# Differential attention in a two-block kernel: the first map left unscaled, the heads held with tokens on partitions, one root and one reciprocal for all heads

## The chip, the cores and the metric

The kernel runs on one core of a Trainium2 chip. The metric is the device time of one execution in microseconds (us). All arithmetic is float32; a large matmul is made of three float32r matmuls on high and low halves of its operands.

## The reference, cut to what matters

The program computes two transformer blocks for 256 latent tokens with 256 context tokens. The change concerns one layer of the first block, differential attention with 8 heads. A head has two score maps (m = 0, 1) of 64 dimensions each and 128 value dimensions. In the reference:

```python
def diff_attend(q, k, v, lam, scale):
    s = jnp.einsum('bqhmd,bkhmd->bhmqk', q, k).astype(jnp.float32) * scale
    p = jax.nn.softmax(s, axis=-1)
    p = p[:, :, 0] - lam * p[:, :, 1]
    return jnp.einsum('bhqk,bkhv->bqhv', p.astype(v.dtype), v)

def out(o):
    o = rms_norm_gain(o, subln_g) * (1.0 - lambda_init)      # over the 128 values of one head, eps 1e-6
    return o.reshape(b, n, DIFF_HEADS * DIFF_DV) @ w_out
```

With e0 and e1 the exponentials of the two maps and s0 and s1 their row sums, the weights of a token are e0/s0 - lam * e1/s1. The norm that follows divides each head's output by its own root mean square, so a factor common to the whole row of a head (such as 1/s0) drops out of it, up to the eps.

## The kernel before, in words

**Program.** The five engines run hand-written streams side by side and meet at semaphores (`S("name")`; `own(...)` issues an instruction and then waits for it on the same engine). Weights come in tiles of 128x1024, one DMA each, through four slots. For every tile ScalarE writes the high half (`hi`, L1159 to L1165), VectorE the low half (`lo`, L1536 to L1540), and then the matmuls may use it. ScalarE reuses a slot of high halves once the matmuls of the tile three before it are done (`tile_done`); the reload of a raw slot waits for the low half (SyncE, L406). `gemm_cols` (L629 to L646) is the output projection: for each of 8 weight tiles k, 8 banks of PSUM get 3 matmuls of 256 columns each. At the end of the last tile each bank is released (`bank_done`), and VectorE adds it to the residual (`residual`, L1611).

**Attention stage.** There are 16 tiles u: 8 heads times 2 blocks of 128 queries. All engines run one software pipeline over u:

- TensorE (L814 to L841): the two score matmuls of tile u (keys 0 to 511 in the free dimension), the four transposes of the mixed map of tile u-2, and the four matmuls with the values of tile u-3. The values are the stationary operand here, so a head's output stands with its 128 value dimensions on partitions and 256 tokens in the free dimension, in bank 6 or 7.
- VectorE (L1844 to L1871): the row maxima of both maps of tile u out of PSUM (L1852), each followed by a small multiply (L1853); then for tile u-1 the reciprocal of both row sums (L1859), the product with -lambda (L1860), the first map scaled by its reciprocal (L1863), and the second map scaled and added (L1864), after which VectorE waits for its own result (L1866). Every second u it also copies a finished head out of PSUM (L1871).
- ScalarE (L1322 to L1336): two exponentials with row sums of tile u, and the copy of the transposed map of tile u-2 from PSUM.

**Norm of the heads.** After the loop, per head: ScalarE squares the head (L1342), TensorE sums over the partitions with a matrix of ones (L846), VectorE scales the 128x256 sums and adds eps (L1877), ScalarE takes the root of 128x256 (L1346), VectorE takes the reciprocal of 128x256 (L1882) and multiplies head, gain and reciprocal (L1883). Then ScalarE rounds the head to the high half (L1349) and GpSimd takes the low half (L500 to L503). The output projection (L849) needs each head only when it comes to its k. `do_var` at 8 (L848) comes before its first matmul.

What follows is the residual, the squares of the next norm, and the second feed-forward layer, whose first weight tiles are converted during the projection.

## Time and profile before

| | |
|---|---|
| device time, median of 3 runs | 3301.37 us (3298.73 to 3304.07) |
| the profiled execution: its own time | 3304.16 us |
| the profiled execution: span | 3302.4 us |
| mean granted clock of TensorE | 0.962 |
| busy share of the span | TensorE 93%, weight load 76%, VectorE 64%, ScalarE 36%, GpSimd 6% |
| attention stage, from the end of the value projection to the first matmul of the output projection | 1077.3 to 1158.2 us of the span |

The span is the time between the first and the last recorded instruction; the own time of that execution is 1.8 us longer. In the tables a line such as L1155 can be that of a helper (all ScalarE activations have it), so the output tile tells instructions apart. PE is TensorE's matmul part and PEld its weight load, DVE is VectorE, ACT ScalarE, POOL GpSimd, SPq the DMA queue of SyncE. The TensorE clock has two levels, and a granted clock of 1.00 is 2.4 GHz and of 0.50 is 1.2 GHz. Float32 matmuls and transposes show as two instructions each.

### The profile page before, as it was taken

How to read it: one execution, taken by the hardware profiler on the slowest of the kernel's cores; microseconds unless marked ns; L12 is line 12 of the kernel's file. 1: busy time of each engine (PE TensorE's matmuls, PEld its weight loads, DVE VectorE, ACT ScalarE, POOL GpSimd, SP SyncE). 2: the span in 40 equal slices, each digit the busy share in tenths (PEclk: the TensorE clock that was granted, in tenths of full speed). 3: DMA queues.
4: the chain of work that ended last, by engine and by line, in shares of the span. 5: the costliest groups of instructions: out<-in, count | busy, mean ns of one | idle time of the engine just before them, and what ended most of it. 6: DMA issues, size and time to landing. Idle time of an engine off the chain costs nothing.

```text
span 3302.4 us, 42571 instructions
## 1 busy us (share of the span) xinstructions
PE 3075.5 (93%) x15288; PEld 2500.8 (76%) x15288; DVE 2099.1 (64%) x3132; ACT 1191.6 (36%) x1756; POOL 199.1 (6%) x171
## 2 busy tenths in 40 slices
PE   6999788999988699999889998999999999998998
PEld 4778466888867489877568886788868777975897
DVE  6972467877686865688589784552258632645654
ACT  3122333332242555364342232442245422412553
POOL 1200000000012000000021120000000000001110
PEclk8999889999999899999999999999999999988999
DMA  6562034666513045511236561673346432533453
GB/s 242 190 212 94 27 132 161 217 202 235 191 64 96 7 151 182 203 52 52 77 119 212 167 203 62 207 246 109 109 159 214 156 114 86 172 113 118 143 185 127
DMA packets 124512, 479.45 MB, mean 145 GB/s; under 512 B 13672, under 2 KB 14696, under 8 KB 121792
## 3 DMA queue, kind: packets, MB, share of 16 engines
q1 hardware_dynamic: 119984, 443.08, 40.3%
q0 software_dynamic: 4368, 34.17, 2.7%
q8 instruction: 109, 1.79, 0.2%
q14 instruction: 51, 0.42, 0.0%
HBM read 459.37 MB, written 17.83 MB: 145 GB/s over the span
## 4 chain that ended last, share of the span: by engine, by line
PE 84%; DVE 10%; issue 3%; ACT 2%; DMA 1%; SPq 0%; DVEq 0%; POOL 0%; ACTq 0%; PEldq 0%
PE bank L576 24%; PE bank L577 24%; PE bank L578 24%; PE bank L1132 2%; PE bank L670 1%; PE bank L725 1%; PE bank L1081 1%; DVE ada_ring_a L1550 1%; DVE diff_rst L1819 1%; DVE tmp L1584 1%; ACT tmp L1155 1%; DVE ada_junk_a L1550 1%; PE bank L676 1%; DVE w_lo L1539 1%; PE bank L712 1%
## 5 line engine op out<-in xcount | busy, mean ns | idle before, releaser
L1539 DVE TENSOR_TENSOR w_lo<-w_raw,w_hi 128x1024 fp32r<-128x1024 f32 x620 | 756.2, 1229 | 733.6 <-ACT w_hi L1155 716.5
L1155 ACT ACTIVATE w_hi<-w_raw 128x1024 fp32r<-128x1024 f32 x623 | 653.7, 1055 | 1050.7 <-PE bank L578 1017.2
L576 PE MATMUL bank<-h_hi,w_hi 128*128 128x512 f32 (+1 forms) x2048 | 727.8, 355 | 65.2 <-DVE h_lo L1603 50.7
L577 PE MATMUL bank<-h_lo,w_hi 128*128 128x512 f32 (+1 forms) x2048 | 720.5, 352 | 0.0
L578 PE MATMUL bank<-h_hi,w_lo 128*128 128x512 f32 (+1 forms) x2048 | 719.4, 351 | 0.0
L576 PEld LDWEIGHTS bank<-h_hi,w_hi 128*128 128x128 f32 x2048 | 393.4, 192 | 127.7 <-issue 69.4
L577 PEld LDWEIGHTS bank<-h_lo,w_hi 128*128 128x128 f32 x2048 | 393.2, 192 | 51.3 <-issue 1.4
L578 PEld LDWEIGHTS bank<-h_hi,w_lo 128*128 128x128 f32 x2048 | 393.0, 192 | 50.7
L576 PE MATMUL bank<-w_hi,xm_hi 128*128 128x512 f32 x512 | 199.5, 390 | 1.7 <-DVE tmp L2081 0.9
L578 PE MATMUL bank<-w_hi,xm_lo 128*128 128x512 f32 x512 | 199.3, 389 | 0.0
L577 PE MATMUL bank<-w_lo,xm_hi 128*128 128x512 f32 x512 | 199.2, 389 | 0.0
L576 PE MATMUL bank<-xm_hi,w_hi 128*128 128x512 f32 (+1 forms) x512 | 173.2, 338 | 1.7 <-issue 0.8
L577 PE MATMUL bank<-xm_lo,w_hi 128*128 128x512 f32 (+1 forms) x512 | 172.7, 337 | 0.0
L578 PE MATMUL bank<-xm_hi,w_lo 128*128 128x512 f32 (+1 forms) x512 | 172.7, 337 | 0.0
L576 PE MATMUL bank<-mlp_hi,w_hi 128*128 128x512 f32 (+1 forms) x512 | 172.0, 336 | 0.0
L577 PE MATMUL bank<-mlp_lo,w_hi 128*128 128x512 f32 (+1 forms) x512 | 172.0, 336 | 0.0
L578 PE MATMUL bank<-mlp_hi,w_lo 128*128 128x512 f32 (+1 forms) x512 | 172.0, 336 | 0.0
L1155 ACT ACTIVATE tmp<-bank 128x512 f32<-128x512 f32 (+1 forms) x124 | 62.3, 502 | 188.4 <-PE bank L578 122.7
L518 POOL TENSOR_TENSOR mlp_lo<-tmp,mlp_hi 128x512 f32 (+1 forms) x64 | 91.4, 1428 | 619.5 <-DVE tmp L2025 574.6
L576 PE MATMUL bank<-ffn_hi,w_hi 128*128 128x512 f32 (+1 forms) x352 | 119.0, 338 | 3.1 <-DVE w_lo L1539 1.7
L578 PE MATMUL bank<-ffn_hi,w_lo 128*128 128x512 f32 (+1 forms) x352 | 118.3, 336 | 0.0
L577 PE MATMUL bank<-ffn_lo,w_hi 128*128 128x512 f32 (+1 forms) x352 | 118.3, 336 | 0.0
(366 smaller groups left out, 4959.2 us busy)
## 6 DMA issues: line engine op xcount, KB each, us to landing
w_raw<-in_weights SPq DMA_DIRECT2D x623, 512.0 KB, 3.5
ada_ring_f<-in_ada SPq DMA_DIRECT2D x56, 512.0 KB, 3.5
ada_ring_g<-in_ada SPq DMA_DIRECT2D x44, 512.0 KB, 3.4
ada_ring_b<-in_ada SPq DMA_DIRECT2D x38, 512.0 KB, 3.6
ada_ring_a<-in_ada SPq DMA_DIRECT2D x32, 512.0 KB, 3.4
ada_first<-in_ada SPq DMA_DIRECT2D x16, 512.0 KB, 16.1
v_spill<-ml_v POOLq DMA_DIRECT2D x1, 4096.0 KB, 11.4
o_spill<-ml_o_grp POOLq DMA_DIRECT2D x4, 1024.0 KB, 4.5
```

Of the source, the lines that this page charges most:

```text
L518: pool.tensor_tensor(mlo[:, t, 0:T], tmp(s % 2, T), mhi[:, t, 0:T].bitcast(F32), SUB)\
L576: mm(out, lhs[0], rhs[0], start=start, stop=False)
L577: mm(out, lhs[0], rhs[1], start=False, stop=False)
L578: return mm(out, lhs[1], rhs[0], start=False, stop=stop)
L670: mm(PS[bank][:, 0:T], ONES[:, :], tmp(3 + c % 2, T), start=c == 0, stop=c == DC - 1)\
L676: last = mm(PS[bank][:, 0:T], ONES[:, :], z[:, c, 0:T], start=c == 0, stop=c == DC - 1)
L712: last = mm(PS[b][:, j * LAT:(j + 1) * LAT], QK[:, 8 + 2 * h + d, key0 + j * P:key0 + (j + 1) * P], QK[:, 2 * h + d, q0:q0 + LAT], start=d ...
L725: last = mm(PS[3 + t][:, :], ATT[:, a, i0:i0 + P], RV[:, v, 512 * h:512 * (h + 1)], start=n == 0, stop=n == len(keys) - 1)
L1132: last = mm(PS[6 + n % 2][:, :], MPT(h, d)[:, j, t * P:(t + 1) * P], MV2[:, j, 512 * h:512 * (h + 1)], start=i == 0, stop=i == len(keys) - 1)
L1155: return nc.scalar.activation(out, in_, func, **kw)
L1539: V.tensor_tensor(WLO[:, slot, :], RAW[:, slot, :], WHI[:, slot, :].bitcast(F32), SUB)\
L1550: ins = V.scalar_tensor_tensor(junk[:, :] if st == 0 else tile, tile, 1.0, rows[:, st, :], MUL, MUL, accum_out=MOD[:, bass.ds(a * 2 + st, 1)])
```

## The change

The change has these parts.

1. **First map unscaled.** VectorE no longer scales the first map. The mixed map is e0 + (-lam * s0/s1) * e1: a reciprocal of s1 alone, one small product `D_MIX`, and one pass over 128x512. The row sums of all 16 tiles are kept (`D_S0`, `D_S1`, 16 columns each). VectorE no longer waits for the mixed map it has just issued. Since the map is s0 times as large as before, the variance gets eps * s0 * s0 (`D_EPS`).
2. **Tokens on partitions.** The operands of the value matmuls are exchanged: the map is stationary and the values move, so a head's output has its tokens on partitions. ScalarE, no longer VectorE, copies it out of PSUM, one tile step later in the pipeline; the loops of both engines grow by two steps.
3. **Norm.** VectorE squares and sums each 128x128 block (tokens x values) in one instruction with an accumulator output (16 of them, inside the pipeline). Then there is one variance, one root and one reciprocal of 128x16 for all heads. ScalarE issues a Sqrt of one column in step 16, ahead of two of its copies.
4. **Scale, turn, split.** VectorE scales 16 blocks of 128x128 by a column, TensorE turns them (16 transposes in 5 turns over banks 4 to 7 and 4 again), ScalarE rounds to the high half with the gain out of PSUM, VectorE takes the low half out of PSUM; GpSimd no longer takes part.
5. **Projection in another order.** Weight tiles 0, 1 and 2 first go to banks 0 to 3, with turns between them; then, once all low halves are there, to banks 4 to 7; tiles 3 to 7 go to all banks as before.

```diff
@@ -205 +205 @@
-        DO = at("diff_o", [P, 8, LAT], ARENA + 40 * K)
+        DO = at("diff_o", [P, 16, DIFF_DV], ARENA + 40 * K)
...
-        DCOL = at("diff_col", [P, 64], ARENA + 88 * K)
+        DCOL = at("diff_col", [P, 192], ARENA + 88 * K)
+        D_S0, D_S1, D_R1, D_MIX, D_SSQ, D_EPS, D_VAR, D_RSTD = (DCOL[:, 32 + 16 * i:48 + 16 * i] for i in range(8))
...
+        DO_TURNS = ((4, (0,)), (5, (1,)), (6, (2, 3)), (7, (4, 5)), (4, (6, 7)))
...
-            for h in range(DIFF_HEADS):
-                pool.wait_ge(S("do_hi_done"), h + 1)
-                pool.tensor_tensor(DOLO[:, h, :], DO[:, h, :], DOHI[:, h, :].bitcast(F32), SUB)\
-                    .then_inc(S("do_lo_done"), 1)
@@ -836 +836 @@
                     if h >= 2:
                         pe.wait_ge(S("d_ocopy"), h - 1)
                     for c in range(4):
-                        last = mm(PS[6 + h % 2][:, t * P:(t + 1) * P], DV[:, c, h * P:(h + 1) * P],
-                                  DPT[:, b % 2, c * P:(c + 1) * P], start=c == 0, stop=c == 3)
+                        last = mm(PS[6 + h % 2][:, t * P:(t + 1) * P], DPT[:, b % 2, c * P:(c + 1) * P],
+                                  DV[:, c, h * P:(h + 1) * P], start=c == 0, stop=c == 3)
                     last.then_inc(S("d_pv"), 1)
-            for h in range(DIFF_HEADS):
-                pe.wait_ge(S("do_sq"), h + 1)
-                if h >= 2:
-                    pe.wait_ge(S("do_var"), h - 1)
-                mm(PS[h % 2][:, 0:LAT], ONES[:, :], tmp(3 + h % 2, LAT), start=True, stop=True)\
-                    .then_inc(S("do_stat"), 1)
-            pe.wait_ge(S("do_var"), 8)
-            gemm_cols("diff_out", LAT, DOHI, DOLO, "do_lo_done", 0)
+
+            def do_turn(i):
+                bank, heads = DO_TURNS[i]
+                if i == 4:
+                    pe.wait_ge(S("do_lo_done"), 1)
+                for h in heads:
+                    pe.wait_ge(S("d_scaled"), h + 1)
+                    for t in range(2):
+                        a = h % len(heads) * LAT + t * P
+                        last = nc.tensor.transpose(PS[bank][:, a:a + P], DO[:, 2 * h + t, :], IDENT[:, :])
+                last.then_inc(S("d_turned"), 1)
+
+            def do_out(k, banks):
+                slot = (FIRST["diff_out"] + k) % SLOTS
+                pe.wait_ge(S("w_lo_done"), FIRST["diff_out"] + k + 1)
+                pe.wait_ge(S("do_lo_done"), k + 1)
+                for o in banks:
+                    last = split_mm(PS[o][:, 0:LAT], w(slot, o * P, P), (DOHI[:, k, :], DOLO[:, k, :]),
+                                    k == 0, k == DC - 1)
+                    if k == DC - 1 and o < DC - 1:
+                        last.then_inc(S("bank_done"), 1)
+                if banks[-1] == DC - 1:
+                    last.then_inc(S("tile_done"), 1)
+
+            for i in range(3):
+                do_turn(i)
+            do_out(0, range(4))
+            do_turn(3)
+            do_out(1, range(4))
+            do_turn(4)
+            do_out(2, range(4))
+            pe.wait_ge(S("do_lo_done"), 8)
+            for k in range(3):
+                do_out(k, range(4, DC))
+            for k in range(3, DC):
+                do_out(k, range(DC))
@@ -1319 +1350 @@
             scale = DIFF_DH ** -0.5
-            for u in range(16 + 2):
+            for u in range(16 + 4):
                 if u < 16:
                     for m in range(2):
                         col = 4 + 2 * (u % 2) + m
@@ -1327 +1358 @@
                         if m == 0 and u >= 2:
                             act.wait_ge(S("d_p"), u - 1)
                         f(DE[:, u % 2, m, :], PS[2 * (u % 2) + m][:, :], ACT.Exp, scale=scale,
-                          bias=DCOL[:, col:col + 1], accum_out=DCOL[:, col + 4:col + 5]).then_inc(S("d_exp"), 1)
+                          bias=DCOL[:, col:col + 1], accum_out=(D_S0, D_S1)[m][:, u:u + 1]).then_inc(S("d_exp"), 1)
+                if u == 16:
+                    f(CELL[:, 1:2], ONES[:, 0:1], ACT.Sqrt)
                 a = u - 2
                 if 0 <= a < 16:
                     act.wait_ge(S("d_tr"), a + 1)
                     if a >= 2:
                         act.wait_ge(S("d_pv"), a - 1)
                     f(DPT[:, a % 2, :], PS[4 + a % 2][:, :], ACT.Copy).then_inc(S("d_pt"), 1)
-            for h in range(DIFF_HEADS + 1):
-                if h < DIFF_HEADS:
-                    act.wait_ge(S("d_ocopy"), h + 1)
-                    if h >= 2:
-                        act.wait_ge(S("do_stat"), h - 1)
-                    f(tmp(3 + h % 2, LAT), DO[:, h, :], ACT.Square).then_inc(S("do_sq"), 1)
-                g = h - 1
-                if 0 <= g:
-                    act.wait_ge(S("do_var"), g + 1)
-                    f(tmp(1 + g % 2, LAT), tmp(1 + g % 2, LAT), ACT.Sqrt).then_inc(S("do_std"), 1)
-            for h in range(DIFF_HEADS):
-                act.wait_ge(S("do_norm"), h + 1)
-                f(DOHI[:, h, :], DO[:, h, :], ACT.Copy).then_inc(S("do_hi_done"), 1)
+                e = u - 4
+                if 0 <= e and e % 2:
+                    h = e // 2
+                    act.wait_ge(S("d_pv"), e + 1)
+                    f(DO[:, 2 * h:2 * h + 2, :].rearrange("p t n -> p (t n)"), PS[6 + h % 2][:, 0:LAT], ACT.Copy)\
+                        .then_inc(S("d_ocopy"), 1)
+            act.wait_ge(S("d_var"), 1)
+            f(D_VAR, D_VAR, ACT.Sqrt).then_inc(S("d_std"), 1)
+            for i, (bank, heads) in enumerate(DO_TURNS):
+                act.wait_ge(S("d_turned"), i + 1)
+                n = len(heads)
+                f(DOHI[:, heads[0]:heads[0] + n, :].rearrange("p h n -> p (h n)"), PS[bank][:, 0:n * LAT], ACT.Copy,
+                  scale=DCOL[:, 1:2]).then_inc(S("do_hi_done"), 1)
@@ -1841 +1874 @@
             scale = DIFF_DH ** -0.5
-            for u in range(16 + 3):
+            for u in range(16 + 5):
                 if u < 16:
                     if u >= 2:
 
@@ -1854 +1887 @@
                             .then_inc(S("d_max"), 1)
                 a = u - 1
                 if 0 <= a < 16:
-                    c = 8 + 2 * (a % 2)
+
                     dve.wait_ge(S("d_exp"), 2 * (a + 1))
-                    own(V.reciprocal(DCOL[:, c + 16:c + 18], DCOL[:, c:c + 2]))
-                    own(V.tensor_tensor(DCOL[:, c + 17:c + 18], DCOL[:, c + 17:c + 18], DCOL[:, 0:1], MUL))
+                    own(V.reciprocal(D_R1[:, a:a + 1], D_S1[:, a:a + 1]))
+                    own(V.scalar_tensor_tensor(D_MIX[:, a:a + 1], D_S0[:, a:a + 1], D_R1[:, a:a + 1], DCOL[:, 0:1],
+                                               MUL, MUL))
                     if a >= 2:
                         dve.wait_ge(S("d_tr"), a - 1)
-                    own(V.tensor_scalar(DP[:, a % 2, :], DE[:, a % 2, 0, :], DCOL[:, c + 16:c + 17], None, MUL))
-                    V.scalar_tensor_tensor(DP[:, a % 2, :], DE[:, a % 2, 1, :], DCOL[:, c + 17:c + 18],
-                                           DP[:, a % 2, :], MUL, ADD).then_inc(S("d_p"), 1)
-                    dve.wait_ge(S("d_p"), a + 1)
-                b = u - 3
-                if 0 <= b < 16 and b % 2:
-                    h = b // 2
-                    dve.wait_ge(S("d_pv"), b + 1)
-                    V.tensor_copy(DO[:, h, :], PS[6 + h % 2][:, 0:LAT]).then_inc(S("d_ocopy"), 1)
-            for h in range(DIFF_HEADS + 1):
-                if h < DIFF_HEADS:
-                    dve.wait_ge(S("do_stat"), h + 1)
-                    if h >= 2:
-                        dve.wait_ge(S("do_norm"), h - 1)
-                    V.tensor_scalar(tmp(1 + h % 2, LAT), PS[h % 2][:, 0:LAT], 1.0 / DIFF_DV, EPS, MUL, ADD)\
-                        .then_inc(S("do_var"), 1)
-                g = h - 1
-                if 0 <= g:
-                    dve.wait_ge(S("do_std"), g + 1)
-                    own(V.reciprocal(tmp(1 + g % 2, LAT), tmp(1 + g % 2, LAT)))
-                    V.scalar_tensor_tensor(DO[:, g, :], DO[:, g, :], DCOL[:, 1:2], tmp(1 + g % 2, LAT), MUL, MUL)\
-                        .then_inc(S("do_norm"), 1)
+                    V.scalar_tensor_tensor(DP[:, a % 2, :], DE[:, a % 2, 1, :], D_MIX[:, a:a + 1],
+                                           DE[:, a % 2, 0, :], MUL, ADD).then_inc(S("d_p"), 1)
+                if a == 15:
+                    V.scalar_tensor_tensor(D_EPS, D_S0, EPS, D_S0, MUL, MUL)
+                e = u - 5
+                if 0 <= e and e % 2:
+                    h = e // 2
+                    dve.wait_ge(S("d_ocopy"), h + 1)
+                    for t in range(2):
+                        n = 2 * h + t
+                        last = V.scalar_tensor_tensor(TMP[:, n * P:(n + 1) * P], DO[:, n, :], 1.0, DO[:, n, :], MUL, MUL,
+                                                      accum_out=D_SSQ[:, n:n + 1])
+                    last.then_inc(S("d_ssq"), 1)
+            dve.wait_ge(S("d_ssq"), 8)
+            V.scalar_tensor_tensor(D_VAR, D_SSQ, 1.0 / DIFF_DV, D_EPS, MUL, ADD).then_inc(S("d_var"), 1)
+            dve.wait_ge(S("d_std"), 1)
+            own(V.reciprocal(D_RSTD, D_VAR))
+
+            def do_scale(h):
+                for n in (2 * h, 2 * h + 1):
+                    last = V.tensor_scalar(DO[:, n, :], DO[:, n, :], D_RSTD[:, n:n + 1], None, MUL)
+                last.then_inc(S("d_scaled"), 1)
+
+            def do_lo(i):
+                bank, heads = DO_TURNS[i]
+                n = len(heads)
+                part = slice(heads[0], heads[0] + n)
+                dve.wait_ge(S("do_hi_done"), i + 1)
+                V.scalar_tensor_tensor(DOLO[:, part, :].rearrange("p h n -> p (h n)"), PS[bank][:, 0:n * LAT],
+                                       DCOL[:, 1:2], DOHI[:, part, :].rearrange("p h n -> p (h n)").bitcast(F32),
+                                       MUL, SUB).then_inc(S("do_lo_done"), n)
+
+            for h in range(4):
+                do_scale(h)
+            do_lo(0)
+            for h in range(4, 6):
+                do_scale(h)
+            do_lo(1)
+            for h in range(6, 8):
+                do_scale(h)
+            for i in range(2, 5):
+                do_lo(i)
```

## Rows read from the trace of the kernel before

**Rows 1.** The page: chain that ended last, share of the span by engine.

```profile
PE 84%; DVE 10%; issue 3%; ACT 2%; DMA 1%; SPq 0%; DVEq 0%; POOL 0%; ACTq 0%; PEldq 0%
```

**Rows 2.** Stretches: us; PE, PEld, DVE, ACT, POOL busy (x); PEclk; DMA; GB/s.

```profile
1091.85:1134.80 42.95, 31.69 (x200) 20.79 (x199) 40.33 (x106) 25.11 (x61) 0.00 (x0) 1.00 0.00 1
...
1138.70:1158.15 19.45, 6.56 (x17) 2.85 (x16) 18.44 (x22) 6.30 (x19) 0.86 (x2) 0.65 0.00 1
1158.15:1161.60 3.45, 3.44 (x16) 3.45 (x17) 3.05 (x3) 1.34 (x5) 3.45 (x5) 0.50 0.00 0
1161.60:1180.10 18.50, 18.50 (x156) 18.50 (x156) 8.90 (x7) 7.39 (x8) 2.50 (x4) 1.00 0.66 228
```

**Rows 3.** Timeline of VectorE in one tile: start us, us, operation.

```profile
1114.46 0.48 DVE L1863 TENSOR_SCALAR diff_p<-diff_e,diff_col 128x512 f32<-128x512 f32 x1
...
1114.98 0.75 DVE L1864 SCALAR_TENSOR_TENSOR diff_p<-diff_e,diff_col,diff_p 128x512 f32<-128x512 f32 x1
1115.76 0.42 DVE L1871 COPY diff_o<-bank 128x256 f32<-128x256 f32 x1
...
1116.11 0.68 DVE L1852 TENSOR_REDUCE diff_col<-bank 128x1 f32<-128x512 f32 x1
```

**Rows 4.** Timeline of TensorE and ScalarE in the same tile.

```profile
1112.52 0.66 PE L829 MATMUL bank<-ident,diff_p 128*128 128x128 f32 x4 [1.00 <-DVE diff_p L1864]
...
1113.41 0.69 ACT L1155 ACTIVATE diff_e<-bank,diff_col 128x512 f32<-128x512 f32 x1 [1.22 <-DVE diff_col L1853]
...
1113.99 0.30 PEld L821 LDWEIGHTS bank<-diff_k,diff_q 64*128 64x128 f32 x4
...
1114.87 0.59 ACT L1155 ACTIVATE diff_pt<-bank 128x512 f32<-128x512 f32 x1
```

**Rows 5.** Timeline of the first tiles, the clock at half until 1090 us.

```profile
1086.02 2.08 PE L821 MATMUL bank<-diff_k,diff_q 64*128 64x512 f32 x4
...
1088.25 1.12 PE L829 MATMUL bank<-ident,diff_p 128*128 128x128 f32 x4 [0.15 <-DVE diff_p L1864]
...
1089.16 1.50 PE L839 MATMUL bank<-diff_pt,diff_v 128*128 128x128 f32 x8
...
1090.59 1.13 PE L821 MATMUL bank<-diff_k,diff_q 64*128 64x512 f32 x4
...
1091.85 0.69 DVE L1852 TENSOR_REDUCE diff_col<-bank 128x1 f32<-128x512 f32 x1 [0.38 <-PE bank L821]
```

**Rows 6.** Chain of waits after the last tile: start us, us, what.

```profile
1138.76 0.42 DVE diff_o L1871
...
1158.16 0.55 PE bank L576
```

**Rows 7.** Groups of VectorE by form, whole run: xcount | busy us, mean ns.

```profile
L1550 DVE SCALAR_TENSOR_TENSOR ada_junk_g<-ada_ring_g,ada_rows_g 128x1024 f32<-128x1024 f32 x44 | 53.6, 1219 | 0.1
...
L1882 DVE RECIPROCAL tmp<-tmp 128x256 f32<-128x256 f32 x8 | 13.9, 1744 | 0.1
...
L1597 DVE TENSOR_SCALAR tmp<-x_res,mod 128x256 f32<-128x256 f32 x16 | 4.8, 346 | 0.0
...
L1821 DVE SCALAR_TENSOR_TENSOR diff_q<-diff_raw,vecs,diff_rst 128x256 f32<-128x256 f32 x8 | 3.9, 485 | 0.3
...
L1550 DVE DVE_READ_ACCUMULATOR ada_junk_a<-ada_ring_a,c_rows 128x1 f32 x32 | 2.6, 82 | 0.0
```

**Rows 8.** Groups by form, 1078 to 1162 us, small operations and copies.

```profile
L1155 ACT ACTIVATE diff_o_hi<-diff_o 128x256 fp32r<-128x256 f32 x8 | 2.8, 404 | 2.1 <-DVE diff_o L1883 2.1
...
L1859 DVE RECIPROCAL diff_col<-diff_col 128x2 f32<-128x2 f32 x16 | 2.5, 155 | 0.0
```

**Rows 9.** Timeline of ScalarE: one later load of a table, and what follows.

```profile
1197.56 1.28 ACT L1155 ACT_TABLE_LOAD   x1
1198.85 1.06 ACT L1155 ACTIVATE w_hi<-w_raw 128x1024 fp32r<-128x1024 f32 x1
```

**Rows 10.** Timeline of ScalarE: the conversion released by the projection's tile 6.

```profile
1180.16 1.06 ACT L1155 ACTIVATE w_hi<-w_raw 128x1024 fp32r<-128x1024 f32 x1 [1.76 <-PE bank L578]
```

## The prediction

> **What bounds the kernel now.** I read the page's chain first: TensorE carries 84% of it and VectorE 10% [rows 1]. So a gain outside TensorE's own work needs a place where TensorE stands and another engine leads. The busy time by stretch finds two such places in the attention stage [rows 2]. In the loop over the tiles (1091.85 to 1134.80 us, tiles 4 to 15) VectorE is busy 40.33 of 42.95 us and TensorE 31.69. From the last value matmul to the first matmul of the projection (1138.70 to 1158.15 us) VectorE is busy 18.44 of 19.45 us and TensorE 6.56. Both times the work is VectorE's and in series: in the loop it goes from one operation to the next without a gap [rows 3], after it the reciprocals of 128x256 lead, 8 at 1.744 us [rows 7]. The weights are no limit here: they lie ready, and after 1161.6 us the projection keeps TensorE full at full clock, 156 matmuls in 18.5 us, 0.119 each [rows 2]. Everything behind the stage hangs on TensorE, so a microsecond won here should reach the end.
>
> **Part 1, the loop.** Per tile VectorE loses the scaling of the first map. Its start to the start of the next operation is 0.52 us [rows 3]. The wait for its own mixed map also goes: a following operation starts 0.07 before the end of the one ahead of it (the copy of 0.42 us has its successor 0.35 after its start), while after the mixed map it starts 0.03 after the end [rows 3]; 0.10 a tile. The small product stays, as a product of three operands. From 1091.85 us to the end of the last mixed map (1134.8) there are 13 such scalings and 12 such waits: 6.76 + 1.20 = 7.96 us off. Six copies of a head lie in that stretch, each 0.35: 2.10 off. They go to ScalarE, 0.40 each [rows 8], which has the room: it is busy 25.11 of 42.95 us [rows 2] and stood idle 1.22 ahead of a tile's exponentials [rows 4].
>
> Added are the squares with a sum, two blocks of 128x128 a head, for five heads before the last tile. Such an operation takes 0.485 at 256 columns [rows 7] and 0.75 at 512 [rows 3], so 0.35 at 128, and 0.28 from one to the next: 5 x 0.56 = 2.80 us on. The read of the accumulator (0.082) [rows 7] overlaps or, as the bound, does not (+0.8). The rows say that the accumulator doesn't slow the pass: 128x1024 with one takes 1.219 against 0.75 for 512 without, 0.92 ns a column [rows 7, 3]. The Trainium skill speaks against this change here: Vector Engine (DVE) Microarchitecture Reference, "Points that are easy to get wrong", says that such an operation with two sources in SBUF that are not bf16 halves its throughput, with no port left for the accumulator. By it each square would take some 0.13 more, 1.3 in the loop and 0.3 behind it, and the sum would be 1.6 smaller; the trace disagrees.
>
> In the first four tiles the clock is at half and TensorE leads: the reduction of tile 4 waits 0.38 for its scores [rows 5]. Of the 4 x 0.62 that VectorE saves there I take 0.7 (bounds 0 and 2.5). Without squares a tile would take VectorE 2.65; TensorE's own ring is scores 1.47 after the transposes' start, and 1.26 from there to the reduction [rows 4, 5], 2.73. So two tiles before the first square lose 0.1 each, 0.25 with the handoffs. Loop: -7.96 - 2.10 + 2.80 - 0.70 + 0.25 = **-7.7 us** (bounds -3 and -9.5).
>
> **Part 2, from the last mixed map to the last value matmul.** This was 1134.79 to 1138.72, 3.93 us. The added Sqrt sits in ScalarE's queue ahead of the copies of tiles 14 and 15. Counted from the start of tile 15's first reduction, ScalarE's first exponential starts at 0.9 (0.69 for the reduction, some 0.2 for its factor), and its copy of the map 1.46 after that [rows 4], at 2.4; with copies of 0.59 and 0.40, which overlap a little, a table load of 1.28 and a root of 0.2, the copy of tile 14 starts at 4.8. VectorE's last mixed map ends at 2.65 + 1.15 = 3.8. So the copy of tile 14 comes 1.0 behind it, tile 15's behind that, and the value matmuls of both tiles run from 1.65 on: 2.0 at full clock (1.47 from transposes to scores [rows 4], less 0.5 for the transposes, is 1.0 a tile) or 3.0 at half (1.50 a tile [rows 5]). That gives 3.7 to 4.7; I take 4.2, **+0.3**. Behind that load nothing more waits for a table. A later load shows what it costs on the queue: 1.28, and the next operation starts 0.01 behind it [rows 9]. The Trainium skill, ScalarE: Activation LUTs, "What ACT_TABLE_LOAD costs", adds a drain of some 1.38 to every switch. By it this part would be 1.4 longer and the sum 1.4 smaller; no gap of that kind follows the load in the trace.
>
> **Part 3, from there to the projection's first matmul.** This was 1138.72 to 1158.16, 19.44 us [rows 6]. New, in series: ScalarE's copy 0.40 [rows 8]; two squares 0.28 + 0.35 + 0.08; the variance on 16 columns 0.16; its root 0.20; the reciprocal of 16 columns, between 0.155 for 2 and 1.744 for 256 [rows 7, 8], 0.24; five handoffs of 0.04. That is 1.91. Then VectorE scales the first four heads: a block of 128x128 is 0.27 (0.346 at 256 columns [rows 7], 0.48 at 512 [rows 3]), 0.20 from one to the next, 8 of them 1.67. The turns of head 0 and its high half lie beside that. Its low half (0.48) comes next, beside turn 2 (four transposes, 0.5 to 0.66 [rows 4]; 1.12 at half clock [rows 5]). With 0.05 that is 4.1: **-15.3 us** (bounds -13.5 and -15.8). Eight reciprocals become one; the eight passes of GpSimd (one of them on the path) and eight matmuls with ones go too.
>
> **Part 4, the projection to the end of tile 6.** I measure to there because the next weight conversion, and with it the residual, is released by it: 1158.16 to 1180.16, 22.0 us for 168 matmuls, of which the first 3.45 us at half clock [rows 2, 10]. New: 168 x 0.119 = 20.0, the turns 3 and 4 in between 0.8, and half clock for a similar time, 1.5. Behind bank 3 TensorE waits for all low halves. VectorE then has 12 scalings and 5 low halves in 7.3 us after the reciprocal (16 x 0.20, 2 x 0.41, 3 x 0.68, and waits), so to 9.2 after the last value matmul; TensorE has 36 matmuls and two turns from 4.1, to 9.2 at full clock, later at half. Cover and covered are level, so I take 0.1. Total 22.4, **+0.4** (bounds -1.5 and +4). Conversions of weight tiles 3 and up come later than in proportion, but tile 3 is ready some 11 us after the last value matmul (1.06 for the high half [rows 10], 1.2 for the low one, behind the low halves of the heads) and wanted at 9.2 + 36 x 0.119 = 13.5. SyncE and GpSimd get no new DMA and no new wait.
>
> **Sum.** -7.7 + 0.3 - 15.3 + 0.4 = **-22.3 us**. Against the profiled execution, 3304.2, that gives 3281.9; it stood 2.8 over the median of 3301.4, so the forecast is **3279.1 us**, 0.7% less. About 0.2%, 6.6 us, is what a measurement of this kernel can tell from no change.
>
> **Rivals.**
> - *The loop keeps its pace*: TensorE's ring or ScalarE (2.6 of work a tile with the copy of a head) becomes the bound, and of part 1 nothing stays. For: TensorE's ring is 2.73 against VectorE's 2.65 to 3.2. Against: both are far below today's 3.4 to 3.6 (42.95 over 12 tiles and the mixing of the last). 3301.4 - 14.6 = 3286.8. Chance 0.15.
> - *The projection trips over its own feed*: TensorE waits for all eight low halves and the clock then halves again. Price: 2 to 3 of waiting, 1.5 of clock, 4 in all: 3283. Chance 0.14.
> - *The clock stays full* from the last tile on, since TensorE no longer stands 19 us: 2.2 more, 3276.9. Chance 0.10.
> - *The clock stays at half* (the other side): in the loop and the projection. A tile then costs TensorE 2.08 + 1.12 + 1.50 = 4.7 [rows 5], 12 of them 56.4 against the 41.3 up to the last mixing: +15.1; the projection 168 x 0.215 (16 matmuls in 3.45 us [rows 2]) + 1.6 against 22.0: +15.7. With part 3 and 0.7 for part 2: +16.2, 3317.6. It decides once the whole projection (15.3 over my part 4) and four tiles (4.7 - 2.9 each, 7.2) run so. Against: TensorE's clock is 1.00 in the loop at a busy share of 0.74 [rows 2], and the share rises. Chance 0.02.
> - *The change doesn't do what it says*: the stage shortens, but what comes behind doesn't start earlier. The chain's DMA share of 1% [rows 1] speaks against. 3301. Chance 0.03.
>
> **How the numbers follow.** The forecast itself has 0.56. The range goes from the full-clock case with a fast loop (3273.5) to the loop rival with a slower part 3 (3289); outside lie the clock rival, no change and some tail. Faster 0.95, same 0.03, slower 0.02.
>
> **What would show it.** Right: two tiles of VectorE in 5.3 without and 5.8 with squares; last value matmul near 1131 us; first projection matmul 4 us behind it; ScalarE's table load between exponentials and copies at 1.28; 168 matmuls and two turns in 22.4. Wrong: reductions that wait for scores; squares over 0.4; scaled blocks over 0.3; TensorE idle ahead of bank 4; later stages that give the time back.

## The result and the profile after

| | before | changed |
|---|---|---|
| device time, median | 3302.03 us (4 runs, 3298.73 to 3304.07) | 3278.78 us (4 runs, 3277.85 to 3279.61) |
| the profiled execution: own time, span | 3304.16, 3302.4 us | 3279.61, 3277.7 us |
| mean granted clock | 0.962 | 0.963 |

The ratio is 0.993, with a 95% interval of 0.9913 to 0.9948: 23 us or 0.7% faster. The forecast was 3279.1. (The median before has a fourth run beside the three that gave 3301.37.)

Busy time by stretch in the changed kernel (in each row start and end, length, then busy time and number of instructions of each engine, the granted clock, the DMA share and GB/s), cut at the same events as in [rows 2]: tile 4's first reduction, end of the last mixed map, end of the last value matmul, first projection matmul, return of the full clock, release by tile 6.

```profile
core 0: us, PE busy (x) PEld busy (x) DVE busy (x) ACT busy (x) POOL busy (x), PEclk, DMA share, GB/s
1093.62:1129.37 35.75, 31.14 (x198) 20.52 (x197) 33.93 (x108) 26.82 (x67) 0.00 (x0) 1.00 0.00 1
1129.37:1132.82 3.45, 2.98 (x25) 2.56 (x23) 1.02 (x10) 2.10 (x5) 0.00 (x0) 1.00 0.00 0
1132.82:1136.77 3.95, 1.62 (x9) 0.84 (x9) 3.14 (x17) 1.47 (x5) 0.00 (x0) 0.98 0.00 0
1136.77:1139.90 3.13, 3.13 (x15) 3.13 (x16) 2.47 (x10) 0.68 (x1) 0.00 (x0) 0.50 0.00 0
1139.90:1159.98 20.08, 19.88 (x165) 19.68 (x165) 10.08 (x9) 8.68 (x9) 0.00 (x0) 1.00 0.48 158
```

The loop went from 42.9 us to 35.75, and TensorE's share in it from 0.74 to 0.87; the stretch in which TensorE stood behind VectorE went from 19.45 to 3.95. The half clock at the projection's start stayed.

VectorE's timeline in the same loop, parts of two tiles (to be compared with [rows 3]). A row has start, duration, engine, line and operation; in brackets stand the idle time before it and who ended it:

```profile
1112.79 0.75 DVE L1897 SCALAR_TENSOR_TENSOR diff_p<-diff_e,diff_col 128x512 f32<-128x512 f32 x1
1113.46 0.29 DVE L1907 SCALAR_TENSOR_TENSOR tmp<-diff_o 128x128 f32<-128x128 f32 x1
1113.67 0.09 DVE L1907 DVE_READ_ACCUMULATOR tmp<-diff_o 128x1 f32 x1
1113.67 0.29 DVE L1907 SCALAR_TENSOR_TENSOR tmp<-diff_o 128x128 f32<-128x128 f32 x1
1113.88 0.09 DVE L1907 DVE_READ_ACCUMULATOR tmp<-diff_o 128x1 f32 x1
1113.88 0.69 DVE L1885 TENSOR_REDUCE diff_col<-bank 128x1 f32<-128x512 f32 x1
...
1115.65 0.22 DVE L1893 SCALAR_TENSOR_TENSOR diff_col<-diff_col 128x1 f32<-128x1 f32 x1
1115.91 0.75 DVE L1897 SCALAR_TENSOR_TENSOR diff_p<-diff_e,diff_col 128x512 f32<-128x512 f32 x1
1116.58 0.69 DVE L1885 TENSOR_REDUCE diff_col<-bank 128x1 f32<-128x512 f32 x1
```

The mixed map now reads both exponentials and the next operation starts 0.67 after its start, 0.08 before its end; before, it started 0.03 behind the end. Two squares take 0.42 us in all, the read of the accumulator lies beside them. Two tiles take 5.80 us instead of 6.87.

ScalarE's timeline at the end of the loop, and TensorE's last value matmuls:

```profile
1128.34 0.38 ACT L1186 ACTIVATE diff_o<-bank 128x256 f32<-128x256 f32 x1
1128.74 1.28 ACT L1186 ACT_TABLE_LOAD   x1
1130.03 0.20 ACT L1186 ACTIVATE cell<-ones 128x1 f32<-128x1 f32 x1
1130.14 1.07 ACT L1186 ACTIVATE diff_pt<-bank 128x512 f32<-128x512 f32 x2
1131.10 0.39 ACT L1186 ACTIVATE diff_o<-bank 128x256 f32<-128x256 f32 x1
1132.86 0.38 ACT L1186 ACTIVATE diff_o<-bank 128x256 f32<-128x256 f32 x1 [1.38 <-PE bank L839]
1134.03 0.22 ACT L1186 ACTIVATE diff_col<-diff_col 128x16 f32<-128x16 f32 x1 [0.79 <-DVE diff_col L1911]
```

```profile
1130.77 2.05 PE L839 MATMUL bank<-diff_v,diff_pt 128*128 128x128 f32 x16 [0.47 <-ACT diff_pt L1186]
1135.11 1.62 PE L852 MATMUL bank<-ident,diff_o 128*128 128x128 f32 x8 [2.28 <-DVE diff_o L1917]
1136.77 0.55 PE L576 MATMUL bank<-diff_o_hi,w_hi 128*128 128x256 f32 x1
```

The load holds the copies of tiles 14 and 15 up, and TensorE waits 0.47 for one. From the last value matmul (1132.82) a chain of small steps leads to the first turn at 1135.11 and to the projection at 1136.77.

**The stage of every run.** Since the whole time also moves with the clock in far-off stages, the runs are compared by the stage too. All times count from the first reduction (which in these profiles lies at 1079.6 to 1082.3 us of the span), read from the timelines. M4 is tile 4's first reduction, P the end of the last mixed map, E of the last value matmul, G the first projection matmul, T the start of the weight conversion that tile 6 releases ([rows 10] before).

| kernel | M4 | M4 to P | P to E | E to G | G to T | T | median, us | before, same job |
|---|---|---|---|---|---|---|---|---|
| before | 11.74 | 42.94 | 3.93 | 19.44 | 22.00 | 100.05 | 3302.03 | |
| changed | 11.34 | 35.75 | 3.45 | 3.95 | 23.21 | 77.70 | 3278.78 | 3302.03 |
| e1_loop_only | 11.38 | 35.43 | 2.77 | 19.43 | 23.00 | 92.01 | 3291.31 | 3299.83 |
| e2_norm_only | 11.74 | 43.11 | 3.86 | 4.00 | 22.58 | 85.29 | 3285.65 | 3299.83 |
| e3_plain_projection | 11.35 | 35.75 | 3.45 | 8.23 | 22.99 | 81.77 | 3281.28 | 3299.83 |
| e4_no_squares_in_loop | 9.86 | 34.89 | 3.46 | 3.95 | 22.62 | 74.78 | 3274.25 | 3299.83 |
| e5_late_table | 9.87 | 35.75 | 2.77 | 4.76 | 22.24 | 75.39 | 3277.34 | 3304.71 |
| e6_squares_scalar | 9.87 | 34.47 | 3.96 | 3.72 | 22.75 | 74.77 | 3274.71 | 3304.71 |
| e7_wait_back | 11.38 | 37.08 | 3.33 | 3.94 | 22.66 | 78.39 | 3277.09 | 3304.71 |
| e8_filler | 11.37 | 35.75 | 3.46 | 4.83 | 21.73 | 77.14 | 3278.28 | 3304.71 |
| c_changed | 11.37 | 35.74 | 3.45 | 3.94 | 23.23 | 77.73 | 3278.36 | 3300.09 |
| e9_squares_shared | 11.35 | 34.31 | 3.45 | 3.94 | 21.74 | 74.79 | 3275.55 | 3300.09 |
| e10_scores_first | 10.43 | 33.47 | 3.45 | 3.94 | 23.11 | 74.40 | 3275.27 | 3300.09 |
| e11_short_filler | 10.45 | 33.45 | 3.46 | 3.94 | 21.75 | 73.05 | 3273.26 | 3300.09 |

### The profile page after: what moved, and what is told of

The parts are those of the page before. It is cut to its first block, busy times and chain, and to the rows that moved or that the text cites. A ratio compares the mean times of both kernels' runs of the same rounds, so it can differ in the third digit from the quotient of the medians.

```text
span 3277.7 us, 42543 instructions
## 1 busy us (share of the span) xinstructions
PE 3071.4 (94%) x15288; PEld 2499.8 (76%) x15288; DVE 2076.9 (63%) x3140; ACT 1188.9 (36%) x1747; POOL 193.2 (6%) x163
## 4 chain that ended last, share of the span: by engine, by line
PE 84%; DVE 9%; issue 3%; ACT 2%; DMA 1%; SPq 0%; DVEq 0%; ACTq 0%; PEldq 0%
PE bank L576 25%; PE bank L577 24%; PE bank L578 24%; PE bank L1163 2%; PE bank L670 1%; PE bank L725 1%; PE bank L1112 1%; DVE ada_ring_a L1583 1%; DVE diff_rst L1852 1%; DVE tmp L1617 1%; ACT tmp L1186 1%; DVE ada_junk_a L1583 1%; PE bank L676 1%; DVE w_lo L1572 1%; PE bank L712 1%
```

## The experiments

**e1_loop_only: part 1 by itself**, made from the kernel before.

```diff
-                    own(V.reciprocal(DCOL[:, c + 16:c + 18], DCOL[:, c:c + 2]))
-                    own(V.tensor_tensor(DCOL[:, c + 17:c + 18], DCOL[:, c + 17:c + 18], DCOL[:, 0:1], MUL))
+                    own(V.reciprocal(DCOL[:, c + 17:c + 18], DCOL[:, c + 1:c + 2]))
+                    own(V.scalar_tensor_tensor(DCOL[:, c + 17:c + 18], DCOL[:, c:c + 1], DCOL[:, c + 17:c + 18],
+                                               DCOL[:, 0:1], MUL, MUL))
...
-                    own(V.tensor_scalar(DP[:, a % 2, :], DE[:, a % 2, 0, :], DCOL[:, c + 16:c + 17], None, MUL))
                     V.scalar_tensor_tensor(DP[:, a % 2, :], DE[:, a % 2, 1, :], DCOL[:, c + 17:c + 18],
-                                           DP[:, a % 2, :], MUL, ADD).then_inc(S("d_p"), 1)
-                    dve.wait_ge(S("d_p"), a + 1)
+                                           DE[:, a % 2, 0, :], MUL, ADD).then_inc(S("d_p"), 1)
```

> The kernel before with part 1 alone: first map unscaled, no wait behind the mixed map; heads, norm and projection as before (the eps is not multiplied by s0 squared). Theory (the parts add up, each on VectorE's path): 13 scalings of 0.52 and 12 waits of 0.12 less, 0.4 in the first tiles: 8.3 us faster, 3293.7; two tiles of VectorE in 5.6 us; the copy of a head stays on VectorE. Rival (the loop's gain is tied to the new norm, or lost to TensorE's own ring and the clock): under 3 us faster, reductions waiting for scores.

3291.31 us (8 runs; the ratio to the kernel before is 0.9973, with an interval of 0.9962 to 0.9983), 8.5 faster than before; the stage is 8.0 shorter. The copy stayed on VectorE, its 0.34 inside a step of 3.02:

```profile
1112.81 0.75 DVE L1864 SCALAR_TENSOR_TENSOR diff_p<-diff_e,diff_col 128x512 f32<-128x512 f32 x1
1113.48 0.42 DVE L1870 COPY diff_o<-bank 128x256 f32<-128x256 f32 x1
1113.82 0.68 DVE L1852 TENSOR_REDUCE diff_col<-bank 128x1 f32<-128x512 f32 x1
```

The loop's gain stands without the new norm; the rival falls. Without the table load in front of the copies P to E is 2.77.

**e2_norm_only: parts 2 to 5 without part 1.**

```diff
+                    own(V.tensor_scalar(DP[:, a % 2, :], DE[:, a % 2, 0, :], D_S0[:, a:a + 1], None, MUL))
                     V.scalar_tensor_tensor(DP[:, a % 2, :], DE[:, a % 2, 1, :], D_MIX[:, a:a + 1],
-                                           DE[:, a % 2, 0, :], MUL, ADD).then_inc(S("d_p"), 1)
-                if a == 15:
-                    V.scalar_tensor_tensor(D_EPS, D_S0, EPS, D_S0, MUL, MUL)
+                                           DP[:, a % 2, :], MUL, ADD).then_inc(S("d_p"), 1)
+                    dve.wait_ge(S("d_p"), a + 1)
...
```

The lines left out give back the reciprocal of both row sums, the two-operand product and the plain eps.

> The changed kernel with the first map scaled again in a pass of its own and with the wait behind the mixed map; heads with tokens on partitions, one root and reciprocal, turns and order of the projection as changed. Theory: the loop gives back 13 x 0.52 + 13 x 0.12 = 8.3 us, the rest stays: 3287.1, and the first projection matmul 4 us behind the last value matmul. Rival (the gains overlap): 3280 or 3295.

3285.65 us (ratio 0.9954, 0.9937 to 0.9970), 14.2 faster than before in its job. M4 to P is back at 43.11, E to G stays at 4.00. The two halves add up: in the stage 8.0 + 14.8 = 22.8 us against 22.35 for both together, in the time 8.5 + 14.2 = 22.7 against 23.2.

**e3_plain_projection: the projection's old order.** All five turns, the wait for all low halves, then `do_out(k, range(DC))` for every k.

> The changed kernel with all five turns first, then the projection tile by tile over all eight banks. Theory: the first projection matmul waits for VectorE's 16 scalings and 5 low halves, 4.6 us later than in the changed kernel; 1.3 comes back (two turns and a wait no longer stand between matmuls): 3.3 us slower, 3282.1. Rival (the order is paid for by half clock and by the waits inside it): within 1 us of the changed kernel.

3281.28 us, 2.5 above the changed kernel (medians of two jobs). In the stage the first matmul comes 4.28 later and T 4.07 later, so only 0.2 of the expected 1.3 came back between G and T. The clock took the rest: in e3 it stays at half until 5.8 us after G, in the changed kernel until 3.1, so 27 matmuls against 12 run at 0.21 us each instead of 0.12. Less the turn that the changed kernel ran at half (0.3), that is some 1.1 us.

```profile
1140.32:1146.10 5.78, 5.78 (x27) 5.78 (x28) 1.22 (x1) 0.29 (x2) 0.00 (x0) 0.50 0.29 92
```

The order is worth its place; the rival falls. Of the 4.1 us some 1.1 are clock, and these profiles don't tell whether the longer stop of TensorE before G (8.23 us) or chance put them there.

**e4_no_squares_in_loop: the squares of heads 0 to 4 left out**, their sums are the constant 128, so the norm of these heads is not computed.

> The changed kernel without the squares of heads 0 to 4 (their sums are a constant). Theory (TensorE's ring comes next behind VectorE): two tiles go from 5.80 to 5.54 us, not to 5.38, reductions wait for scores: 1.3 us faster than the changed kernel, 3277.5. Rival (VectorE alone sets the pace): 5.38 a pair, 2.1 us faster.

A pair of tiles takes 5.57 us. The timeline shows a reduction that starts 0.18 later than VectorE's own sequence (0.67 behind the mixed map's start) would let it:

```profile
1109.95 0.75 DVE L1898 SCALAR_TENSOR_TENSOR diff_p<-diff_e,diff_col 128x512 f32<-128x512 f32 x1
1110.80 0.69 DVE L1886 TENSOR_REDUCE diff_col<-bank 128x1 f32<-128x512 f32 x1
```

M4 to P fell by 0.86, less than either number; 0.35 of what is missing is one tile, whose reduction at 1105.23 waited 0.43 us for its scores. That TensorE's ring (from the transposes over the value matmuls and the scores to the reduction and the mixed map, and back) comes next fits, but this run alone doesn't show that it is the ring; e10 does. The median, of another job, fell by 4.5 us. The stage of the profile accounts for 2.9 of it: 0.9 in the loop, 1.5 in M4, where the half clock fell elsewhere (see below), and 0.6 in the projection.

**e5_late_table: the early Sqrt behind the last copy of a head.**

> The changed kernel with ScalarE's early Sqrt moved from ahead of the last two copies of the map to behind the last copy of a head. Theory (a load costs 1.28 us on the queue and nothing more): the copies of tiles 14 and 15 start 1.3 us earlier, the last value matmul ends 0.9 earlier, the load then lies beside VectorE's squares and pushes the root back by 0.6: 0.3 us faster, 3278.5. Rival (the Trainium skill, ScalarE: Activation LUTs, What ACT_TABLE_LOAD costs: load and drain 2.66 us): the root comes 1.4 later than that, 1.1 us slower.

ScalarE's timeline:

```profile
1128.01 0.38 ACT L1186 ACTIVATE diff_o<-bank 128x256 f32<-128x256 f32 x1 [0.97 <-PE bank L839]
1128.41 1.28 ACT L1186 ACT_TABLE_LOAD   x1
1129.70 0.20 ACT L1186 ACTIVATE cell<-ones 128x1 f32<-128x1 f32 x1
1129.81 0.20 ACT L1186 ACTIVATE diff_col<-diff_col 128x16 f32<-128x16 f32 x1
```

P to E fell by 0.68 and E to G rose by 0.81: level, 0.1 slower where I expected 0.3 faster. The load starts 0.02 behind the copy, takes 1.28, and the next operation starts 0.01 later. So the further 1.38 us of drain that the Trainium skill, ScalarE: Activation LUTs, "What ACT_TABLE_LOAD costs", gives for a switch did not appear, neither here, with the queue waiting for the load, nor in the changed kernel.

**e6_squares_scalar: all squares on ScalarE, out of PSUM.** Here and in e9 to e11 VectorE also waits for its `D_EPS`.

```diff
+                    for t in range(2):
+                        n = 2 * h + t
+                        last = f(TMP[:, n * P:(n + 1) * P], PS[6 + h % 2][:, t * P:(t + 1) * P], ACT.Square,
+                                 accum_out=D_SSQ[:, n:n + 1])
+                    last.then_inc(S("d_ssq"), 1)
```

> The changed kernel with the squares and their sums on ScalarE, straight out of PSUM, for all heads. Theory: VectorE's pair falls to 5.38 us but TensorE's ring holds it at 5.54, ScalarE is busy 5.3 of it; 1.3 us less in the loop, 0.2 more behind it (two squares of 0.49 and the copy in series on ScalarE): 1.1 us faster, 3277.7. Rival (ScalarE becomes the bound and delays the copies of the map): the pair stays at 5.8 or above, no gain.

M4 to P is 34.47, 1.3 less, with a pair at 5.55; P to G is 7.68 against 7.40. Together 1.0 faster from M4 to G, 1.1 expected. The price came elsewhere than I put it: ScalarE squares head 5 ahead of the table load, and so the last value matmul comes 0.5 later.

**e7_wait_back: `dve.wait_ge(S("d_p"), a + 1)` put back behind the mixed map.**

> The changed kernel with VectorE's wait for its own mixed map put back. Theory: 0.10 to 0.12 us a tile, 1.4 us slower, 3280.2; the operation behind the mixed map starts 0.03 after its end instead of 0.08 before. Rival (the wait is free, since the reductions wait for scores anyway): nothing.

M4 to P rose by 1.33, which is 12 x 0.11; the operation behind the map starts 0.79 after its start instead of 0.67:

```profile
1112.11 0.75 DVE L1897 SCALAR_TENSOR_TENSOR diff_p<-diff_e,diff_col 128x512 f32<-128x512 f32 x1
1112.90 0.29 DVE L1908 SCALAR_TENSOR_TENSOR tmp<-diff_o 128x128 f32<-128x128 f32 x1
```

The median, 3277.09, is 1.7 below the changed kernel's first one. A term of 1.3 us can be read from the stage, and cannot be read from medians of different jobs.

**e8_filler: four matmuls of 128x512 with unused results, between the last value matmul and the first turn.**

```diff
+            for j in range(4):
+                mm(PS[j % 4][:, 0:512], ONES[:, :], DV[:, j % 4, 0:512], start=True, stop=True)
```

> The changed kernel with four added matmuls of 128x512 (ones by values, into banks 0 to 3, results unused) between the last value matmul and the first turn. Theory (the half clock at the projection's start comes from TensorE standing some 4 us ahead of it): the granted clock stays 1.00 into the projection, its first 12 matmuls take 1.4 us instead of 2.7, 1.3 us faster, unless the added work (over 2.3 us) delays the first turn. Rival (the half clock comes from the thin load of the last tiles, or moves by itself from run to run): the clock halves all the same, 0 to 1 us slower.

They took 3.60 us and delayed the first turn, E to G rose by 0.88. But the granted clock stayed 1.00 and G to T fell by 1.48. Net 0.6 shorter in the stage, and 0.5 in the median, within the spread of the runs. So the filler should be shorter, which e11 tries.

**c_changed: the changed kernel again**, in the job of the next three.

> The changed kernel itself once more, beside the three that follow, to see how far its time and its stage move from job to job. Theory: stage times to 0.1 us as before wherever the clock is full (M4 to the last mixed map 35.75, from there 3.45 and 3.95), the first tiles and the projection move by up to 1.5 us with where the half clock falls; time 3278.8 within 1.5.

3278.36 us (5 runs, 3276.35 to 3279.32); all five parts of its stage are within 0.03 of the first time.

**e9_squares_shared: squares of heads 0 to 4 on ScalarE, of 5 to 7 on VectorE**, with e6's instructions on ScalarE.

> The changed kernel with the squares of heads 0 to 4 on ScalarE out of PSUM and those of heads 5 to 7 on VectorE as changed. Theory (TensorE's ring holds a pair at 5.55, and the squares on ScalarE cost only behind the loop): 1.3 us less from tile 4 to the last mixed map, 3.45 and 3.95 behind it unchanged: 1.3 us faster than the changed kernel. Rival (ScalarE's longer steps delay the copies at the end): behind the loop 0.5 more.

M4 to P 34.31, 1.4 less than c_changed; P to E and E to G unchanged at 3.45 and 3.94. G to T was also 1.5 shorter, because the half clock did not come at the projection in this profile, although TensorE stands there as long as in c_changed. From E to G and behind it:

```profile
1131.06:1135.00 3.94, 1.61 (x9) 0.83 (x9) 3.14 (x17) 1.48 (x5) 0.00 (x0) 1.00 0.00 0
1135.00:1138.10 3.10, 3.10 (x26) 3.10 (x27) 2.64 (x11) 1.36 (x2) 0.00 (x0) 1.00 0.00 0
```

Of the 2.9 us by which the stage is shorter 1.4 is the squares and the rest the clock, which here nothing in the edit was meant to move. The median is 3275.55 (3273.68 to 3276.14), 2.8 below c_changed, with no run in common; in how many of the unprofiled runs the clock stayed up is not known.

**e10_scores_first: e9, and TensorE's loop in the order scores of tile u, value matmuls of u-4, transposes of u-2.**

```diff
-            for u in range(16 + 3):
+            for u in range(16 + 4):
...
-                b = u - 3
+                b = u - 4
```

> As e9, and TensorE issues the scores of the next tile ahead of the value matmuls of the tile three back. Theory (the ring is transposes, value matmuls, scores; without the value matmuls in it scores come 1.0 us earlier): no reduction waits for scores, a pair falls to VectorE's 5.38, 1.0 us less in the loop than e9 and up to 1 less in the first tiles: 2.3 to 3.3 faster than the changed kernel. Rival (something else holds the pair at 5.55, ScalarE or the hand-over of the map): no difference to e9.

VectorE's timeline:

```profile
1108.76 0.75 DVE L1903 SCALAR_TENSOR_TENSOR diff_p<-diff_e,diff_col 128x512 f32<-128x512 f32 x1
1109.43 0.68 DVE L1891 TENSOR_REDUCE diff_col<-bank 128x1 f32<-128x512 f32 x1
...
1114.14 0.75 DVE L1903 SCALAR_TENSOR_TENSOR diff_p<-diff_e,diff_col 128x512 f32<-128x512 f32 x1
```

No reduction waits any more; a pair takes 5.37 us. M4 to P is 0.84 less than in e9 and M4 0.92 earlier. With the squares gone and only the order changed the pair went from 5.54 to 5.37, so what held it was the ring from the transposes over the value matmuls to the scores. The median, 3275.27 (3273.34 to 3280.03), is that of e9. In the profile the projection ran at half clock here, G to T 23.11 against 21.74, and the whole stage is 0.4 shorter than e9's.

**e11_short_filler: e10 with two filler matmuls.**

> As e10, with two added matmuls of 128x512 (results unused) behind the last value matmul. Theory: they take 1.8 us, less than TensorE stands there, so the first turn is not delayed (E to G 3.95), the clock stays 1.00 into the projection and its first 12 matmuls take 1.5 us: 1.3 us faster than e10. Rival (two are too few): half clock as before, same time as e10.

Stretches of e10 and then of e11 around the projection's start (1131.46 and 1131.44 us):

```profile
1129.00:1131.40 2.40, 1.60 (x8) 0.85 (x8) 2.36 (x11) 0.86 (x2) 0.00 (x0) 0.93 0.00 0
1131.40:1134.50 3.10, 3.10 (x15) 3.07 (x15) 2.53 (x10) 0.69 (x1) 0.00 (x0) 0.50 0.00 0
```

```profile
1127.40:1129.80 2.40, 1.83 (x6) 0.53 (x5) 1.50 (x9) 0.60 (x2) 0.00 (x0) 1.00 0.00 0
1129.80:1131.40 1.60, 1.60 (x8) 0.79 (x8) 1.60 (x8) 0.86 (x2) 0.00 (x0) 1.00 0.00 0
1131.40:1134.50 3.10, 3.06 (x26) 3.09 (x27) 2.65 (x11) 1.38 (x2) 0.00 (x0) 1.00 0.02 5
```

The two kernels stand at the same moment and issue the same matmuls; with two fillers ahead the clock is 1.00 and 26 of them touch the 3.1 us instead of 15. The first turn is not delayed, G to T falls by 1.36 as expected, T is at 73.05. That the fillers kept the clock up is likely and not shown: both profiles with them (e8 and this one) stay at 1.00 from E on. Of the ten with the turns and without fillers nine have the half clock somewhere between E and 6 us behind G, and one, e9, has none. The median is 3273.26 us (3272.60 to 3276.89), 5.1 below c_changed in the same job, whose fastest run was 3276.35; the ratio to before is 0.9916 (0.9902 to 0.9929) against 0.9930 (0.9917 to 0.9944), so the intervals overlap. The stage is 4.7 us shorter than c_changed's, of which 2.3 is the loop, 0.9 the first tiles and 1.5 the clock.

## Why the prediction was right

The forecast of 3279.1 us against 3278.78 is closer than its steps. Term by term in the stage:

- **Part 1, the loop:** -7.7 forecast, -7.6 measured (7.19 after tile 4, 0.40 before it; the 0.40 hangs on where the half clock falls, for e5, with the same instructions there, has M4 at 9.87). e1 and e7 bear out the pass of 0.52 and the wait of 0.10, which measures 0.11. Two errors cancel: the small product costs 0.22 instead of 0.16, 0.26 from its start to the next, 0.8 us over 13 tiles, which I had put at nothing; the squares take 0.21 from one to the next instead of 0.28, 0.7 us less over five heads. The accumulator read overlaps. As for the halved throughput that the Trainium skill, Vector Engine (DVE) Microarchitecture Reference, "Points that are easy to get wrong", gives for such an operation with two float32 sources in SBUF: 0.289 us for 128 columns, against the 0.48 that halving would make of my estimate, shows none of it. TensorE's ring, sized at 2.73 a tile, measures 2.77 (e9) and is gone in e10.
- **Part 2, to the last value matmul:** +0.3 forecast, -0.5 measured. The step that failed is the start of the copy of tile 14 "1.0 behind" the last mixed map's end; it measures 0.77 (1130.14 against 1129.37), and the clock was full here where it was half before, so the value matmuls of two tiles took 2.05 (the 2.0 of my own bound) and not the middle of 2.0 and 3.0. e1 and e5 price the table load in this place at 3.45 - 2.77 = 0.7 us.
- **Part 3, to the projection:** -15.3 forecast, -15.5 measured, 3.95 instead of 4.1. The squares were again the term too large. e2 shows that it needs nothing of part 1. Which of parts 2 to 4 won how much was not tried; that the reciprocals led is read from the profiles, 13.9 us for eight of 128x256 before [rows 7] and one of 128x16 in 0.25 now.
- **Part 4, the projection to tile 6:** +0.4 forecast, +1.2 measured. The half clock cost 1.4 to 1.5 (e8, e9 and e11 run without it: 21.74), near the 1.5 taken. The wait for all low halves was TensorE's stop from the last matmul on bank 3 (1143.36) to the next (1143.84), 0.36 more than the usual 0.12, not 0.1. It is the same at full clock (e9: 1140.13 to 1140.60), so it isn't the clock: the last turn comes only ahead of the last 12 matmuls on these banks, and they, 1.44 us, don't cover its high half (0.69) and its low half (0.75) with the handoffs. The prediction had weighed all of VectorE's work against all of TensorE's and missed this tail. The turns took 1.0 with one of them at half clock (0.7 in e9), not 0.8; the rest is 0.12 a matmul instead of 0.119, restarts behind each stop, and 0.2 at the end, from the last matmul to the conversion, which the forecast's sum left out. e3 confirms that the order pays all the same: 4.1 us, some 1.1 of it clock.

In sum -22.35 against -22.3: part 2 was 0.8 too pessimistic and part 4 0.8 too optimistic, by chance the same. And with the half clock where it fell in e5's first tiles the same instructions would have given -23.8.

The rivals: the loop that keeps its pace falls with e1 and the changed profile. TensorE's ring was there, but under VectorE's time as long as the squares were in it. The projection's own feed cost 0.4 and not 4. The clock that stays full did not occur in the changed kernel; e9 and e11 show what it is worth where it does, 1.4 to 1.5, of my 2.2. The clock at half throughout did not occur: the first stretch above is at 1.00.

What the stage doesn't account for: the span fell by 24.7 us. The stage began 2.2 later in the changed profile, and what follows T was 4.5 shorter. The record gives no ground to put either down to the change.

Ahead of the stage all fourteen profiles run the same instructions, and its start goes with the time that the granted clock was at its lower level before it, summed from the traces: 99.0 us in six profiles (before, e5, e6, e7, e10, e11), with the start at 1079.58 to 1080.98; 102.4 us in four (e2, e3, e4, e8), 1081.05 to 1081.55; 105.8 us in four (changed, c_changed, e1, e9), 1081.95 to 1082.30.

Behind T the instructions are the same too. This part took 2122.2 us before, 2117.7 in both profiles of the changed kernel, and from 2115.9 (e5) to 2121.8 (e11) in the experiments, so it moves by 5.9 among the kernels with an edit, none of which touches it. Half clock adds up to 126.7 us there before and to 127.2 in the changed profile: it is not how much of it there is. Where it falls differs. Stretches of the kernel before, then of the changed one at about the same point of its work:

```profile
1600.00:1620.00 20.00, 18.11 (x73) 14.45 (x73) 15.90 (x41) 7.76 (x10) 0.00 (x0) 0.91 0.17 51
1640.00:1660.00 20.00, 17.75 (x47) 8.84 (x46) 13.83 (x33) 3.88 (x8) 0.00 (x0) 0.91 0.34 131
```

```profile
1578.50:1598.50 20.00, 18.73 (x83) 15.14 (x82) 14.40 (x39) 6.66 (x9) 0.00 (x0) 1.00 0.25 75
1618.50:1638.50 20.00, 15.79 (x38) 6.17 (x36) 11.70 (x29) 7.08 (x11) 0.00 (x0) 1.00 0.32 124
```

Whether such places make up the 4.5 us stays open.

## What to carry to other kernels

Where an engine stands behind a chain of full-width elementwise passes, move the statistic to the layout in which it is one number per partition: eight reciprocals of 128x256 became one of 128x16, and 19.4 us became 4. When two engines run close in a software pipeline, shortening the leader exposes the ring through the other: look at the order of the other's work first (e10: the same matmuls, 0.17 us a pair). Read terms of a microsecond from the stage in the profile and not from medians of different jobs: e7 was 1.3 us slower there and 1.7 us faster in the median.

## What the runs showed of the hardware that I had not expected

- The half clock moves from profile to profile on the same stretch of work. In the first tiles it ended early enough to put M4 at 9.87 (e4, e5, e6) or late enough for 11.35 (changed, e3, e7, e8, c_changed, e9), 1.5 us apart with the same instructions or nearly so. The start of the whole stage moved by 2.7 us in the same way. At the projection the changed kernel ran its first 3 us at 0.50 both times; e9, which stood there for as long, ran them at 1.00.
- Unused work may be worth its time: with some 1.8 us of filler matmuls in a gap where TensorE stood anyway the clock was 1.00 behind it, and 1.36 us were saved against e10. e9 had the full clock there without them, so one profile of each doesn't prove the fillers.
- A square of a 128x128 block with its sum took 0.289 us, less than the 0.35 that 0.485 at 256 and 0.75 at 512 columns led to.
- A three-operand operation on a single column took 0.220 us where the two-operand one of the same size took 0.16; in 13 tiles in series that made 0.8 us.
